# A hybrid transformer layer on one core: an opening reordered, rows stored in another channel order, one expert's tokens turned earlier, the last product taken in another loop order

## What is computed

```python
mod = silu(cond) @ w_ada + b_ada            # six vectors: shift1 scale1 gate1 shift2 scale2 gate2
h = modulate(rmsnorm(x, norm1), sh1, sc1)
z = h @ w_in                                # q, k, v (12 heads) and u (512)
attn = attention(q, k, v)                   # windows for latents, full for context
ssm = s5_readout(s5_states(u))              # discretised state space model, then GLU
x = x + g1 * (concat(attn, ssm) @ w_out)
h = modulate(rmsnorm(x, norm2), sh2, sc2)
aff = softmax(h @ w_router)                 # expert choice: each expert takes its best tokens
g, idx = top_k(aff.T, cap)                  # 64 latent and 16 context tokens for each of 16 experts
xs = h[idx]
y = (silu(xs @ w_gate) * (xs @ w_up)) @ w_down * g
x = x + g2 * scatter_add(y, idx)
```

## Time and profile before

| | us |
|---|---|
| three timed runs | 2528.22, 2522.69, 2524.87 |
| their median | 2524.87 |
| the profiled execution's own time | 2518.89 |
| span of the profile | 2517.1 |
| PE busy, share of the span | 2342.5, 93% |
| DMA, mean rate | 250 GB/s |

### The profile page before, as it was taken

The page is one execution under the profiler, slowest core; times in us unless marked ns, Lnnn a source line. Parts: engine busy times, 40 slices in busy tenths (PEclk is TensorE's granted clock), DMA queues, the critical chain, the costliest instruction groups (busy, mean ns, idle before and its releaser), DMA issues.

```text
span 2517.1 us, 56866 instructions
## 1 busy us (share of the span) xinstructions
PE 2342.5 (93%) x26284; PEld 1531.0 (61%) x26284; DVE 573.1 (23%) x886; ACT 333.9 (13%) x710; POOL 272.2 (11%) x370
## 2 busy tenths in 40 slices
PE   4999999999999999999999489999999989999996
PEld 2468888555555556554445476667676666666662
DVE  4124432244444433421013400000000000000001
ACT  3012111022222233310012100000000000000000
POOL 3046770000000000000110000000000000000000
PEclk9999999999999999999999599999999999999998
DMA  9932213856556411232422899999999999999994
GB/s 342 352 88 78 66 48 80 271 184 224 198 174 206 137 55 55 79 144 99 161 100 112 284 345 386 394 396 397 395 404 406 399 396 396 395 395 391 398 403 157
DMA packets 207607, 628.75 MB, mean 250 GB/s; under 512 B 14058, under 2 KB 90564, under 8 KB 152388
## 3 DMA queue, kind: packets, MB, share of 16 engines
q1 hardware_dynamic: 189120, 585.04, 61.2%
q0 software_dynamic: 3072, 20.97, 3.6%
q10 hardware_dynamic: 15188, 19.19, 2.3%
HBM read 600.72 MB, written 24.44 MB: 248 GB/s over the span
## 4 chain that ended last, share of the span: by engine, by line
PE 70%; DMA 20%; DVE 4%; ACT 2%; issue 2%; ACTq 1%; SPq 0%; POOL 0%; DVEq 0%; POOLq 0%
PE PS L1489 15%; PE PS L1308 14%; PE PS L1399 11%; DMA work<-in_w_gate 9%; DMA hT_<-in_w_gate 8%; PE PS L1124 7%; PE PS L1503 7%; PE PS L1071 3%; PE PS L1006 3%; DVE work L1781 2%; PE PS L1336 2%; DMA work<-in_w_down 1%; PE PS L1296 1%; PE PS L1033 1%; PE PS L1321 1%
## 5 line engine op out<-in xcount | busy, mean ns | idle before, releaser
L1489 PEld LDWEIGHTS PS<-hT_,work 128*64 128x64 f32 x14336 | 515.6, 139 | 99.2 <-issue 54.4
L1489 PE MATMUL PS<-hT_,work 128*64 128x80 f32 x14336 | 534.1, 236 | 45.0 <-DMA work<-in_w_gate 21.6
L1308 PE MATMUL PS<-hT_,work 128*128 128x512 f32 (+1 forms) x1536 | 440.6, 437 | 0.0
L1308 PEld LDWEIGHTS PS<-hT_,work 128*128 128x128 f32 x1536 | 224.3, 191 | 157.5 <-issue 157.5
L1503 PE MATMUL PS<-work,hT_ 128*32 128x512 f32 (+1 forms) x2544 | 298.7, 596 | 3.3 <-DMA work<-in_w_down 2.0
L1399 PE MATMUL PS<-work,mixT_ 128*128 128x512 f32 x640 | 280.7, 599 | 0.0
L1896 DVE TENSOR_TENSOR hT_<-PS,hT_ 128x480 f32<-128x480 f32 x16 | 10.5, 657 | 955.7 <-ACT hT_ L989 955.7
L1124 PE MATMUL PS<-work,hT_ 128*128 128x256 f32 x960 | 214.4, 382 | 0.6 <-DMA work<-in_w_in 0.6
L1399 PEld LDWEIGHTS PS<-work,mixT_ 128*128 128x128 f32 x640 | 122.3, 193 | 149.6 <-issue 149.6
L1124 PEld LDWEIGHTS PS<-work,hT_ 128*128 128x128 f32 x960 | 181.6, 191 | 26.6 <-issue 1.2
L1503 PEld LDWEIGHTS PS<-work,hT_ 128*32 128x32 f32 (+1 forms) x2544 | 71.7, 105 | 143.4 <-issue 128.9
(11 more groups left out here) (251 smaller groups left out, 1722.3 us busy)
## 6 DMA issues: line engine op xcount, KB each, us to landing
work<-in_w_up SPq DMA_DIRECT2D x57, 2048.0 KB, 27.1
work<-in_w_down SPq DMA_DIRECT2D x56, 2048.0 KB, 36.8
work<-in_w_gate SPq DMA_DIRECT2D x55, 2048.0 KB, 33.7
work<-in_w_ada SPq DMA_DIRECT2D x48, 2048.0 KB, 11.2
work<-in_w_in SPq DMA_DIRECT2D x80, 512.0 KB, 4.7
hT_<-in_w_gate SPq DMA_DIRECT2D x9, 2048.0 KB, 37.0
work<-in_w_out SPq DMA_DIRECT2D x4, 4096.0 KB, 13.3
hT_<-in_w_down SPq DMA_DIRECT2D x8, 2048.0 KB, 31.4
```

Source lines behind the costliest of these rows:

```text
L1308: last = pe.matmul(bank(2 * which, n, col), w_chunk[chunk % NW][:, HD * (k % 8):HD * (k % 8) + HD], hT[:, k, col:col + n], start=(k == 0), ...
L1489: last = pe.matmul(hidden_at(u, f)[64 * h:64 * h + 64, :], w[:, k % 4, f * P + 64 * h:f * P + 64 * h + 64], xsT[s][:, k, :], start=opens, ...
```

## The change

1. **Opening.** On ACT, square sums and roots of x come before the discretisation; tiles 0 and 1 share one root instruction, tiles 2 to 4 another. On DVE the discretisation becomes a function called in front of group 1 of the loop. `Q` moves to the start of the work memory, so that SP's wait before `ring(3)` goes; the scratch for the squares and POOL's clearing of 16 columns of `X_` move to suit. PE turns tiles 0 and 1, runs `ada(0, 0)`, turns tiles 2 to 4, then `columns(0, 0)`, `ada(0, 1)`, `columns(0, 1)`. `powers_turned` and ACT's copies of them move from group 0 to group 1.
2. **Channel order.** `norm` reads every second channel and writes the even and the odd channels of each 256 side by side; the router's weights are loaded in the same order; `turn_four` reads 128 adjacent channels. Counts of instructions stay.
3. **Tokens of expert 1.** Its four `turn_four` follow `gate_up(0, 1)`, `(0, 3)`, `(0, 5)` and `(0, 7)`; ACT copies them out before `hidden(0)`.
4. **Last down.** k becomes the outer loop for k = 0 to 5, bank c the inner; k = 6 and 7 follow for each bank.

```diff
-        at(31240 - 22 * P)
+        at(0)
         Q = take(22 * P, 64).rearrange("p (n h s) -> p n h s", n=22, h=2)
...
-            sp.wait_ge(s_tabT, 3)
             ring(3)
...
+            act.wait_ge(s_pcol, 3)
+            for part, s_, tiles in ((0, s_xa, (0, 1)), (1, s_xb, (2, 3, 4))):
+                act.wait_ge(s_, 16)
+                for i in tiles:
+                    if i:
+                        act.wait_ge(s_xsum, i)
+                    act.activation(x_junk, x_rows[i], ACT.Square, accum_out=small[:, 16 + i:17 + i]).then_inc(s_xsum, 1)
+                act.wait_ge(s_xsum, tiles[-1] + 1)
+                act.activation(small[:, 24 + tiles[0]:25 + tiles[-1]], small[:, 16 + tiles[0]:17 + tiles[-1]], ACT.Sqrt,
+                               bias=eps[:, :], scale=1 / D).then_inc(s_xss, 1)
+            for i in (3, 4):
...
             act.wait_ge(s_rows, 80)
             act.activation(r_tmp[0][:, 0:1], ldt, ACT.Exp).then_inc(s_ract, 1)
...
             context_scaled(0)
+            context_scaled(1)
             powers_out(0, D9)
             powers_out(1, I9)
-            context_scaled(1)
+            context_scaled(2)
...
             tokens_out(0, 0)
+            tokens_out(1, 1)
             hidden(0)
-            tokens_out(1, 1)
...
+            turn_x(0)
+            turn_x(1)
             pe.wait_ge(s_ct, 1)
-            for part in range(2):
-                ada(0, part)
-                columns(0, part)
+            ada(0, 0)
+            for i in range(2, TT):
+                turn_x(i)
+            columns(0, 0)
+            ada(0, 1)
+            columns(0, 1)
             pe.wait_ge(s_xev, 8)
...
-                if g == 0:
-                    powers_turned(0, 0, 8, 2)
+                if g == 1:
+                    powers_turned(0, 0, 8, 4)
...
-                    rows = xs[s][:, k // NEAR * NEAR * P:(k // NEAR + 1) * NEAR * P].rearrange("t (p i) -> t i p", i=NEAR)
-                    last = turn(bank(7, SLOTS, (k - 4 * b) * SLOTS), rows[:, k % NEAR, :], SLOTS)
+                    last = turn(bank(7, SLOTS, (k - 4 * b) * SLOTS), xs[s][:, k * P:(k + 1) * P], SLOTS)
...
+            pe.wait_ge(s_gath[0], 16)
+            for b in range(4):
+                turn_four(0, 0, b)
+            pe.wait_ge(s_xsev, 4)
+            for j in range(8):
+                gate_up(0, j, j, 0)
+                if j % 2 == 1:
+                    if j == 1:
+                        pe.wait_ge(s_gath[1], 16)
+                    turn_four(1, 1, j // 2)
...
+            for k in range(6):
+                if k % 2 == 0:
+                    landed(12 * EXPERTS - 4 + k // 2, 0)
+                for c in range(3):
+                    if k == 0:
+                        pe.wait_ge(s_ye, START + 6 * (EXPERTS - 2) + 2 * c + 2)
+                    last_down(k, c)
+            landed(12 * EXPERTS - 1, 0)
             for c in range(3):
...
+                last_down(6, c)
+                last_down(7, c).then_inc(s_used, 1)
...
             for g in range(4):
+                if g == 1:
+                    discretised()
                 for part in range(2):
...
-                for half in range(2):
-                    cols = slice(half * D // 2, (half + 1) * D // 2)
-                    ch.mark(STT(h2[tt % 2][:, cols], x1[:, tt, cols], stat[:, tt, 1:2], scale2[:, c, cols], ALU.mult, ALU.mult))
+                rows = h2[tt % 2].rearrange("t (b i p) -> t i b p", p=P, i=NEAR)
+                natural = [x.rearrange("t (b p i) -> t i b p", p=P, i=NEAR) for x in (x1[:, tt, :], scale2[:, c, :], shift2[:, c, :])]
+                for i in range(NEAR):
+                    ch.mark(STT(rows[:, i], natural[0][:, i], stat[:, tt, 1:2], natural[1][:, i], ALU.mult, ALU.mult))
```

More of the change, by code:

```diff
@@ L671, in _ @@
             act.activation(cT_wide[:, :, 0:2], turned.rearrange("p (c k) -> p k c", c=2), ACT.Silu).then_inc(s_ct, 1)
+            act.wait_ge(s_pcol, 3)
[10 more added lines that the diff above has]
+                for b in range(4):
+                    act.wait_ge(s_xt, 4 * i + b + 1)
+                    act.activation(hT[:, 4 * b:4 * b + 4, i * P:(i + 1) * P], bank(b).rearrange("p (k t) -> p k t", k=4),
+                                   ACT.Copy).then_inc(s_xev, 1)
             act.wait_ge(s_rows, 80)
@@ L1011, in _, with turn_x @@
             turn(bank(7, 32, 64), crow, 32).then_inc(s_pt, 1)
-            for i in range(TT):
+            def turn_x(i):
                 pe.wait_ge(s_xn, i + 1)
@@ L1045, in columns @@
                     pe.wait_ge(s_ct, 1)
-                if g == 1:
+                if g == 2:
                     pe.wait_ge(s_tab, 2 + 2 * part)
-                elif g == 2 and part == 0:
+                elif g == 3 and part == 0:
                     pe.wait_ge(s_tab, 10)
@@ L1531, in _ @@
+            pe.wait_ge(s_xsev, 4)
[5 more added lines that the diff above has]
+                    turn_four(1, 1, j // 2)
             for e in range(1, EXPERTS):
                 expert(e, e % 2, 12 * e - 4, 0, 16 * ((e + 1) // 2 + 1) if e + 1 < EXPERTS else None)
-            pe.wait_ge(s_hh, START + 2 * EXPERTS)
-            for c in range(3):
-                pe.wait_ge(s_ye, START + 6 * (EXPERTS - 2) + 2 * c + 2)
-                for k in range(8):
-                    r = 12 * EXPERTS - 4 + k // 2
-                    if c == 0 and k % 2 == 0:
-                        landed(r, 0)
-                    w = w_ring[r % RING].rearrange("p (k n) -> p k n", k=2)
-                    for g, first, n, col in ((0, 0, 32, c), (1, 32, 32, c), (2, 64, 16, c), (3, 32 * c, 32 if c < 2 else 16, 3)):
-                        last = pe.matmul(bank(3 + c)[32 * g:32 * g + n, :], actT[1][:, k, first:first + n],
-                                         w[:, k % 2, col * BANK:(col + 1) * BANK], start=(k == 0), stop=(k == 7))
-                last.then_inc(s_used, 1)
@@ new lines, in last_down @@
+            def last_down(k, c):
+                w = w_ring[(12 * EXPERTS - 4 + k // 2) % RING].rearrange("p (k n) -> p k n", k=2)
+                for g, first, n, col in ((0, 0, 32, c), (1, 32, 32, c), (2, 64, 16, c), (3, 32 * c, 32 if c < 2 else 16, 3)):
+                    last = pe.matmul(bank(3 + c)[32 * g:32 * g + n, :], actT[1][:, k, first:first + n],
+                                     w[:, k % 2, col * BANK:(col + 1) * BANK], start=(k == 0), stop=(k == 7))
+                return last
@@ L1620, in _ @@
             x_norm(1)
-            for i in range(3):
-                x_turned(i)
-                x_norm(i + 2)
+            x_turned(0)
+            x_norm(2)
+            x_turned(1)
+            x_norm(3)
+            x_norm(4)
+            x_turned(2)
             for g in range(4):
+                if g == 1:
+                    discretised()
                 for part in range(2):
@@ L1832, in norm @@
                     dve.wait_ge(s_h2T, 4 * (tt - 1))
[L1833 to L1835 removed]
+                rows = h2[tt % 2].rearrange("t (b i p) -> t i b p", p=P, i=NEAR)
+                natural = [x.rearrange("t (b p i) -> t i b p", p=P, i=NEAR) for x in (x1[:, tt, :], scale2[:, c, :], shift2[:, c, :])]
+                for i in range(NEAR):
+                    ch.mark(STT(rows[:, i], natural[0][:, i], stat[:, tt, 1:2], natural[1][:, i], ALU.mult, ALU.mult))
                 ch.wait()
[L1837 to L1839 removed]
+                for i in range(NEAR):
+                    TT_(rows[:, i], rows[:, i], natural[2][:, i], ALU.add).then_inc(s_h2, 1)
             def route(tt):
```

130 lines of the change are left out of this document (52 added, 78 removed).

## The result

The changed kernel takes 2509.7 us (median of 9 runs, 2499.29 to 2518.25), the kernel before, run beside it, 2523.98 (9 runs, 2518.32 to 2528.39). The ratio is 0.9946, with an interval of 0.9928 to 0.9965: 13.6 us faster, 9 to 18 by the interval. The forecast was 2509.6.

What follows compares the result with a forecast made beforehand. The weights' transfer was taken to bound most of the experts' stage, but not the opening or the last product. Terms -7.7 + 0 + 0.5 - 8.1 = -15.3 from the median 2524.87 gave 2509.6 us, range 2501 to 2518.

Steps and rivals of the forecast that it cites:

- Opening: Start of the kernel through the u_blocks: square sums and ada(0, 1) come earlier; -7.7 us, bounds -9.5 and 0.
- piece 3: Opening: the piece of w_ada that ada(0, 1) needs, taken to land at about 42.0 us.
- the wait for the context blocks: Opening, u_block(0): fifth matmul waits for context_scaled(0) in ACT's queue; 1.1 us in one case, nothing otherwise, counted zero.
- Rival (a): Opening: gain doesn't arrive, POOL's rows for Q or the context blocks being late; gain 2, 2515 us; chance 0.13.
- Channel order: Norm and turns: reading every second float costs DVE nothing; 0, from -0.5 to +4.9 us.
- rival (b): Norm: reads of every second float run at a fraction of the rate; slower, 2559 us at 1/f = 4; chance 0.04.
- Tokens of expert 1: Expert 0 to expert 1: turns moved into expert 0's gate and up, silu's load exposed; +0.5 us, bounds -1.7 and +1.2.
- the issue behind expert 1's start: Experts: the piece SP issues at 1505.67, which hangs on PE, sets the saturated run of transfers to the end.
- Last down: Last product: PE goes on from 2474.92 without pause and ends at 2496.9; -8.1 us, bounds -6.5 and -8.5.
- rival (c): Last product: PE's lower clock or alternating banks cost time; gain 3 instead of 8, 2514.5 us; chance 0.07.
- The sign that I gave: End of the kernel: no PE gap above 1.6 us from 2460 on, shifted by 7.
- Rival (d): Routing and expert 1: PE's slow starts vanish with the shift, more gain than forecast; 2504 us; chance 0.07.

Runs made afterwards that it cites:

- e8: The changed kernel with 32 products of 128 x 128 into an unused bank put into PE's queue at its wait for piece 3; 2511.5 us, ratio 0.9957.
- e7: The changed kernel with pieces 2 and 3 of w_ada issued ahead of the first two chunks of w_in; 2503.92 us, ratio 0.9918.
- e9: The changed kernel with w_ada's pieces 2 and 3 first and the second expert's tokens in their old place; 2502.28 us, ratio 0.9923.
- e4: The kernel before with the channel order alone; 2519.46 us, ratio 0.9995.
- e12: The changed kernel with a one-element square root ahead of the first expert's silu, adding a second table load; one execution, 2509.59 us.
- E0: Not a run: the start of expert 0's first gate and up; from it to expert 1's first gate and up, 48.30 us before, 48.56 after.
- e2: The kernel before with the last down by blocks alone; 2513.08 us, ratio 0.9963.
- e6: The changed kernel with one element put through silu between the copies of expert 0's and expert 1's tokens; 2504.62 us, ratio 0.9932.
- e5: The changed kernel with the second expert's tokens turned where they were before, behind the whole first gate and up; 2508.77 us, ratio 0.9947.
- e1: The kernel before with the opening's edits alone; 2518.06 us, ratio 0.9985.

## Why the prediction was right, and which of its terms were not

**The total** was met to 0.1 us, and that is luck. The steps as measured are -4.4, 0, +2.0 and -8.0, together -10.4 where I had -15.3. The four parts alone give 3.8 - 3.3 + 9.3 + 1.3 = 11.1 by their ratios. The measured 13.6 has both in its interval, and 15.3 as well.

**Opening, -7.7 forecast, -4.4 found.** The first half of the working held: what is late next is piece 3; the second half of `ada(0, 0)` began at 28.43, when piece 1 landed (28.5 forecast); the dry spell is gone; the turns of `Q` begin with no wait; the wait for the context blocks is nothing beside a slow start and 0.60 beside a fast one (1.1 forecast). The step that failed is the sum from the landing on. The piece came at 42.86, not 42.0: 0.9. The second half of `ada(0, 1)` took 2.76, not 1.8: 0.9. The columns took 1.86, not 1.05: 0.8. The first ten instructions took 6.93, and I had left them at 6.14: 0.8. Together 3.4, all of the miss (3.3): the first `u_block` started at 49.21, not 46.6, and the last ended at 151.31, not 148.0. The landing was misread to begin with: before, the transfers were at full rate to 41.0 and at a DMA share of 0.29 from 41.2 to 41.4, so they ran dry near 41.3, and piece 3 of the changed kernel landed 1.5 later than that. The pieces behind it, which have slots now, travel at the same time; that this is why it comes later was not tested. PE's wait was off too. I had three tiles of x paced by four copies each, 8.1 us; with ACT copying beside DVE their turns took 5.64, so PE was ready at 38.56 and stood still for 4.3 us, where my sum left it under 1. So I had moved the steps to a place where PE stands still just before them, and costed them with durations from a place where it hadn't; I knew of the slow start of PE but put it only where it already stood. e8 shows that the clock was the cause of the three slow steps, e7 and e9 that the landing was the bound.

**Rival (a)** came half true, with another mechanism than POOL or the context blocks.

**Channel order, 0 forecast, 0 found** (e4). The row of L1682 was the right one to go by, and rival (b) is dead. The turns got cheaper by 0.2 per group of four, not 0 to 0.1; it moves nothing that can be measured.

**Tokens of expert 1, +0.5 forecast, +2.0 found.** The stretch from the last gate and up to expert 1 was 3.98 (4.1 forecast), with the table load of 1.28 exposed in it and no drain: the copy ends at 1474.62, the load starts at 1474.63, silu at 1475.92. The 1.38 us of drain that the Trainium skill, "ScalarE: Activation LUTs", section "What ACT_TABLE_LOAD costs", would have added didn't appear, here or at the two loads of e12; the measurement decides. That the turns slip into PE's pauses also held: E0 to E1 isn't longer. The step that failed is that I ended the sum at expert 1's first instruction. Behind it 2.3 us were lost, 1.5 of them to pauses that the old order didn't have. I had noted these pauses ("issue") and counted on them only as room.

**That the issue behind expert 1's start sets the run to the end** held in fourteen profiles, with the issue spread over 20 us and the rest over 3.4.

**Last down, -8.1 forecast, -8.0 found** in the profile and 9.3 (5.8 to 12.9) in e2. The count of steps was right to 0.2 us; rival (c) is dead. The sign that I gave, no gap of PE above 1.6 us, was not met: there is one of 1.79 ahead of the last down, a wait for DVE. A gap of 1.75 stood in the same place before, so it costs nothing new.

**Rival (d)** didn't show: expert 1 began with a slow start as before, the routing of the last tile ran at 0.50 in both profiles, and in the opening the slow stretch grew longer.

## What to carry to other kernels

When a step is moved behind a wait, cost it also at the lower clock, which PE may have after that wait, not only with the duration from its old place; and ask first whether the wait can go by giving the transfer a better place in its queue, which was worth 3.7 us here for a change of two lines. A pause that the profile gives to nobody isn't free room: see whether its distance, counted in instructions, is constant, and carry the sum on until the next point at which the stage is bound again. Where parts of a change are below 0.2% each, one profile of a whole kernel can't weigh them; distances within a stage over several profiles can.

## What the runs showed of the hardware that I had not expected

- PE's instruction stream is itself a transfer, one packet for some 256 instructions. While the weights were being loaded, pauses of up to 2.15 us stood at distances of one packet; they sit at fixed places in the stream (moved by 64 and 32 by as many products put in ahead), and three in a row came 6.20 us after the one before.
- The place at which the granted clock fell to 0.50 differs between executions of the same opening. In the changed kernel (4.3 us of waiting) and in e6 (3.5) it fell about 1 us after work had begun again, in e5 (3.2) as it began, in e1 (3.1) at 43.0, 0.1 before it began, and in e12 (3.3) not before 48.5.
- Four turns of 80 x 128 took 0.70 us with their operand read at every second float and 0.50 with adjacent floats, while DVE's reads of 1024 elements took 1.24 us either way.
- A table load took 1.28 us, and at most 0.02 lay between it and the operations on either side, alone or twice in a row.
